# Four products of an input block in alternating order: wide of block one, narrow of two, wide of two, narrow of one

## The reference: what is computed

```python
h = rmsnorm(x, norm1_w[l])
proj = jnp.einsum('bsd,dp->bsp', h, w_in[l])
(aq, ak, av, z, xbc, dt_raw, m_qk, m_v, m_o, m_i, m_f) = split_columns(proj, PROJ_SIZES)
y_att = moba_attention(aq, ak, av)        # after per-head rmsnorm of aq, ak
y_ssm = mamba2_ssd(z, xbc, dt_raw, ...)
y_mlstm = mlstm_chunkwise(m_qk, m_v, m_o, m_i, m_f, ...)
x = x + jnp.einsum('bsm,md->bsd', jnp.concatenate([y_att, y_ssm, y_mlstm], axis=-1), w_out[l])
h = rmsnorm(x, norm2_w[l])
gate, val = jnp.split(jnp.einsum('bsd,df->bsf', h, w_up), 2, axis=-1)
x = x + jnp.einsum('bsf,fd->bsd', gelu(causal_dwconv(gate)) * val, w_down)
```

## Time and profile before

| | |
|---|---|
| median of 3 runs | 409.44 us (409.28 to 409.79) |
| profiled execution, its span | 407.5 us |
| PE | 402.4 us busy, 99% of the span, 2257 matmuls |
| PE's weight load | 345.9 us, 85% |
| DVE | 305.0 us, 75% |
| ACT | 263.2 us, 65% |
| POOL | 48.0 us, 12% |
| DMA | 74.09 MB, 182 GB/s on average |

### The profile page before, as it was taken

One profiled execution on the slowest core, in us unless ns is written; L12 is line 12 of the kernel. 1 busy time (PEld: TensorE's weight loads), 2 busy tenths in 40 slices (PEclk: granted clock), 3 DMA queues, 4 the chain that ended last, 5 costly groups with the idle time before them and its releaser, 6 DMA issues.

```text
span 407.5 us, 6020 instructions
## 1 busy us (share of the span) xinstructions
PE 402.4 (99%) x2257; PEld 345.9 (85%) x2257; DVE 305.0 (75%) x445; ACT 263.2 (65%) x363; POOL 48.0 (12%) x30
## 2 busy tenths in 40 slices
PE   8999999999999999999999999999999999999996
PEld 8988888788888888888888888888888888888885
DVE  4989869777666889879766778976777667776775
ACT  6979889884499865897536575555554565535540
POOL 3107975410011000000004000000000000000000
PEclk9999999999999999999999999999999999999999
DMA  8845764674453522236554256555445555355202
GB/s 308 340 166 191 276 258 158 250 229 178 139 236 117 195 103 105 103 125 237 194 180 195 105 190 224 206 185 216 166 155 210 202 206 193 128 208 198 97 2 103
DMA packets 12644, 74.09 MB, mean 182 GB/s; under 512 B 1336, under 2 KB 2768, under 8 KB 4432
## 3 DMA queue, kind: packets, MB, share of 16 engines
q1 hardware_dynamic: 12616, 73.81, 50.1%
q10 hardware_dynamic: 8, 0.00, 0.0%
HBM read 72.74 MB, written 1.07 MB: 181 GB/s over the span
## 4 chain that ended last, share of the span: by engine, by line
PE 98%; DMA 1%; DVE 0%; ACT 0%; issue 0%; ACTq 0%
PE pj L1536 25%; PE pj L1537 14%; PE pj L1496 8%; PE pj L1498 8%; PE pj L1497 8%; PE mx L1561 6%; PE mx L1497 6%; PE mx L1498 6%; PE mx L1496 6%; PE pj L1539 4%; PE mx L1558 2%; PE mx L1536 2%; PE mx L1537 1%; DMA x_pad<-in_x 1%; PE pj L1606 1%; PE pj L1614 0%
## 5 line engine op out<-in xcount | busy, mean ns | idle before, releaser
L925 DVE TENSOR_TENSOR wlo<-w_b,whi 128x2048 fp32r<-128x2048 f32 x55 | 125.9, 2290 | 46.0 <-ACT whi L453 46.0
L1536 PE MATMUL pj<-hT,whi 128*128 128x512 f32 x434 | 153.8, 396 | 0.0
L453 ACT CAST whi<-w_b 128x2048 fp32r<-128x2048 f32 x63 | 120.2, 1908 | 27.7 <-PE pj L1498 22.0
L1537 PE MATMUL pj<-hT,wlo 128*128 128x256 f32 x496 | 133.9, 280 | 0.0
L1536 PEld LDWEIGHTS pj<-hT,whi 128*128 128x128 f32 x434 | 81.4, 188 | 18.6 <-issue 0.5
L1537 PEld LDWEIGHTS pj<-hT,wlo 128*128 128x128 f32 x496 | 93.6, 189 | 2.4
L413 POOL TENSOR_TENSOR wlo<-w_b,whi 128x2048 fp32r<-128x2048 f32 x8 | 37.1, 4642 | 117.2 <-ACT whi L453 97.1
L841 ACT COPY st_b<-pj 128x512 f32<-128x512 f32 x22 | 12.9, 587 | 41.2 <-PE pj L1539 41.2
L1496 PE MATMUL pj<-whi,hT 128*128 128x512 f32 x96 | 38.2, 398 | 0.0
L1498 PE MATMUL pj<-whi,hT 128*128 128x512 f32 x96 | 37.5, 390 | 0.0
L1497 PE MATMUL pj<-wlo,hT 128*128 128x512 f32 x96 | 37.4, 389 | 0.0
(11 more groups left out here) (288 smaller groups left out, 611.2 us busy)
## 6 DMA issues: line engine op xcount, KB each, us to landing
w_b<-in_w_in SPq DMA_DIRECT2D x23, 1024.0 KB, 4.9
w_b<-in_w_up SPq DMA_DIRECT2D x22, 1024.0 KB, 4.8
w_b<-in_w_down SPq DMA_DIRECT2D x11, 1024.0 KB, 4.8
w_b<-in_w_out SPq DMA_DIRECT2D x8, 1024.0 KB, 4.8
seg_b<-ld_rows SPq DMA_DIRECT2D x4, 512.0 KB, 6.5
x_pad<-in_x SPq DMA_DIRECT2D x2, 512.0 KB, 3.8
w_b<-in_w0c SPq DMA_DIRECT2D x1, 512.0 KB, 6.0
Wm_b<-m_rows_d SPq DMA_DIRECT2D x1, 512.0 KB, 5.6
```

Source lines behind the costliest of these rows:

```text
L453: nc.scalar.copy(whi[:, slot, :], wraw[:, slot, :]).then_inc(s.hi_done, 1)
L925: nc.vector.tensor_tensor(wlo[:, slot, :], wraw[:, slot, :], whi[:, slot, :].bitcast(F32), ALU.subtract).then_inc(s.lo_done, 1)
L1536: nc.tensor.matmul(ps, whi[:, slot, w], hT[:, k, :, :], start=k == 0, stop=False, skip_group_check=True)
L1537: ins = nc.tensor.matmul(ps[:, 0:T], wlo[:, slot, w], hT[:, k, 0, :], start=False, stop=False, skip_group_check=True)
```

## The change: what it does

In `pairs` each input block k had, for both output blocks j in turn, wide then narrow, into the same bank (for the last block, k = 7, narrow then wide). Now each k has wide of j = 0, narrow of j = 1, wide of j = 1, narrow of j = 0, and k = 7 is no exception.

```diff
                     for j in range(2):
-                        w = slice(k * 256 + j * P, k * 256 + (j + 1) * P)
-                        ps = home[:, j * 512:(j + 1) * 512]
-                        if k < KD - 1:
-                            nc.tensor.matmul(ps, whi[:, slot, w], hT[:, k, :, :], start=k == 0, stop=False, skip_group_check=True)
-                        ins = nc.tensor.matmul(ps[:, 0:T], wlo[:, slot, w], hT[:, k, 0, :], start=False, stop=False, skip_group_check=True)
-                        if k == KD - 1:
-                            ins = nc.tensor.matmul(ps, whi[:, slot, w], hT[:, k, :, :], start=False, stop=True, skip_group_check=True)
+                        wide, narrow = (slice(k * 256 + i * P, k * 256 + (i + 1) * P) for i in (j, 1 - j))
+                        nc.tensor.matmul(home[:, j * 512:(j + 1) * 512], whi[:, slot, wide], hT[:, k, :, :],
+                                         start=k == 0 and j == 0, stop=k == KD - 1 and j == 1, skip_group_check=True)
+                        ins = nc.tensor.matmul(home[:, (1 - j) * 512:(1 - j) * 512 + T], wlo[:, slot, narrow], hT[:, k, 0, :],
+                                               start=k == 0 and j == 0, stop=k == KD - 1 and j == 1, skip_group_check=True)
```

## The result

The changed kernel takes 410.64 us (median of 9 runs, 410.56 to 411.01) against 409.67 for the kernel before (9 runs, 409.28 to 410.10). The ratio is 1.0029 with a 95% interval of 1.0019 to 1.0038: slower by 0.29%, 1.2 us by the ratio; the two medians as they stand differ by 0.97. The profiled execution has a span of 408.6 us, against 407.5.

What follows compares the result with a forecast made beforehand. PE's pace, from matmul start to start, was taken as the bound. Steps +0.9, first five units +0.2, 56 pairs -0.1 and single units 0 gave +1.0 us on the 409.44 median: 410.4 us, range 407.3 to 411.3.

Steps and rivals of the forecast that it cites:

- Count of work: In the 31 units of pairs: no matmul, weight load, DMA or wait is added, removed or moved; cost 0.
- banks: New order of banks in the pairs: the bank of a matmul seems to change nothing; taken as 0.
- end of the unit: `unit_done` now comes from a narrow; results end within 0.01 us of before and PE doesn't wait for the reader; cost 0.
- all-fast rival: Wide and narrow meeting in one bank make the slow pace, so the new order makes all pairs fast; 407.5 us, chance 0.15.
- still slower one: Rival: narrow and next wide sharing a bank cost 6.6 ns more a pair; +3.3 to +5 us, 413 to 414, chance 0.05.
- The odd order takes a slow stream into a fast unit, and without it a stream keeps its pace: At the seam of units: without the odd order, a step's 32 pairs keep their entry pace, slow 353.3 ns against fast 346.7.
- Nine steps, +0.9: Steps from 248.49 on: all 32 pairs slow, 11.29 us instead of 11.20, plus `down`'s entry; +0.9 us (0.6 to 1.1).
- term for `down`'s entry: In each of nine steps, `down` entered from a slow stream loses one more slow wide; +0.01 us (-0.02 to +0.03).
- First five units, +0.2: First 80 pairs, entered from narrows, all slow: 28.27 us instead of 28.06; +0.2 us.
- the 56 pairs, -0.1: Pairs from 223.40 to 243.03, begun fast, stay fast: 19.50 us instead of 19.63; -0.1 us.
- Seven single units, 0 within -0.4 and +0.3: Units alone between transposes, four slow and three fast before: pace open, all slow +0.3, all fast -0.4, taken as 0.
- no change of pace: Rival: something else at the seam sets the pace, so units keep alternating slow and fast; 409.1 to 409.4 us, chance 0.20.

Runs made afterwards that it cites:

- banks alone: Kernel before with the new order of banks and the old order of widths, k = 7 included; 409.79 us, ratio 1.0005.
- widths alone: Kernel before with wide then narrow for all eight k, the order of banks as before; 410.81 us, ratio 1.0028.
- k = 0 odd: Against the kernel with the odd order at k = 1 of `pj0` in nine steps: moved to k = 0; 408.85 us, ratio 0.9981 to the kernel before.
- narrow first: Against the kernel with the odd order at k = 1: narrow then wide in every pair of the nine steps; 410.77 us, ratio 1.0037 to the kernel before.

## Why the prediction was right, and one term that was too small

*PE's pace bounds the kernel.* Right: nothing but distances between PE's starts changed. Beside the pairs' pace the prediction set the Trainium skill's formula (TensorE: Matmul & The Clock Gate, section Back-to-back issue gap) without its condition: the section gives it for a matmul on its own. The pairs here come every 346.7 or 353.3 ns against 325 by it. No term of the sum rests on it.

*Count of work, banks, end of the unit: 0 each.* Right. The banks alone gave 1.0005 and the same step to 0.01 us; the value chosen from the earlier trace rows held, and with it fell the all-fast rival and the still slower one. The end of the unit was not tested by itself; no view shows a wait of PE in the steps, before or after.

*The odd order takes a slow stream into a fast unit, and without it a stream keeps its pace.* Shown from both sides: without it all 32 pairs are slow (widths alone, 16.80), with it at k = 1 all behind it are fast (16.59). The prediction left out that the point matters. At k = 3 the same odd order changes nothing, 1.46 us more for the same work. The kernel before had its k = 7 at a point that works, in nine steps of nine; by its trace alone only the first unit of `pairs`, slow on both sides of its odd end, would have told it. An odd place can also do the opposite: in the kernel before the third unit of `pairs` is fast, and behind its odd end the fourth is slow (39.72 on).

*Nine steps, +0.9.* The 32 pairs were right, 11.29. The term for `down`'s entry was too small: taken as +0.01 with +0.03 as its upper bound, it measured 5.50 - 5.46, +0.04. The estimate took one more slow wide; in fact ten matmuls instead of six pass before the stream settles (276.54 to 278.87 is 2.33 against 2.27). Measured for nine steps: 9 x 0.13 = +1.2, above this term's own range of 0.6 to 1.1.

*First five units, +0.2, and the 56 pairs, -0.1.* Right to 0.01 us each (28.27; 19.50).

*Seven single units, 0 within -0.4 and +0.3.* Near 0, and in part by luck: the prediction had no reason for a pace here. By the traces four are slow and three fast again, but not the same ones. The unit at 64.3 turned fast (a mean of 397 for its wides instead of 404, -0.09), the one at 162.7 slow (404 instead of 399, +0.10); up to k = 7 both have the same sequence of widths as before, entered behind the same transposes. Another 0.14 was won at 57.7 and the transposes behind it, some 0.08 of it (0.31 - 0.23) because PE now reaches them behind the end of `xdt_b` (63.54 and 63.35) and no longer waits. Up to 223.4 the changed kernel is 0.09 us behind (223.49 against 223.40), with the same start of its first pair to 0.01: the five units' +0.2 less these 0.1.

The sum by the trace is +1.2 for the steps, -0.1 for the 56 pairs and +0.1 up to 223.4, +1.2 in all; the medians' ratio says +1.2, forecast was +1.0. The rival "no change of pace" is out too: its trace would have had the mean of 391 in `pj1`.

## What to carry to other kernels

Where PE is busy without a gap, read its pace from start to start over ten or more matmuls, not from busy time: two stretches of the same shapes may differ by 2%. An irregular spot in the code, such as another order for the last block, may be what keeps the pace; before it is tidied away, look at the pace on both sides of it. If a stream is slow from its entry, try one break of its pattern at each of the first few places, and count what was won only where no other engine takes it back.

## What the runs showed of the hardware that was not expected

Wide and narrow matmuls with a weight load each have two paces when they alternate, 346.7 and 353.3 ns a pair, with the same shapes, the same order of banks and the same granted clock. The pace is set at the entry or at a break, and it held for 80 pairs (28.27 us for the five units). The sequence of widths there is not all that sets it: the same sequence ran slow in one execution and fast in another (12 pairs in 4.24 and 4.16 us), where its first pair was 0.03 us longer, and the unit at 64.3 was slow before and fast after the change (means of 404 and 397 ns). A single place where two wides follow each other can switch it (k = 0 odd against narrow first: steps of 16.60 and 16.79 us). The odd order switches it at k = 1 and, the same break two input blocks later, not at k = 3 (11.11 and 11.29 us for the 32 pairs). A stream of wides alone always settles at 226.7 ns, but loses up to 0.06 us on the way, by its entry (5.45, 5.46, 5.48 and 5.50 us for the same 24 matmuls). What in TensorE holds this state was not found; no run here tried other widths or other dtypes.
